# Second attention: a pair's early shares are multiplied ahead of its context maxima

## The reference, cut to what matters

```python
s_ctx = jnp.einsum('bqgrd,bkgd->bgrqk', qb, kc).astype(F32) * scale
s_win = jnp.einsum('bqgrd,bkgd->bgrqk', qb, kb).astype(F32) * scale
s_win = jnp.where(valid, s_win, -jnp.inf)
p = softmax_with_sink(jnp.concatenate([s_ctx, s_win], axis=-1), sink).astype(v.dtype)
return (jnp.einsum('bgrqk,bkgd->bqgrd', p[..., :C], vc)
        + jnp.einsum('bgrqk,bkgd->bqgrd', p[..., C:], vb))
...
sc = jnp.einsum('bqgrd,bkgd->bgrqk', qc, kc).astype(F32) * scale
pc = softmax_with_sink(sc, sink).astype(vc.dtype)
oc = jnp.einsum('bgrqk,bkgd->bqgrd', pc, vc).reshape(b, C, Q_DIM)
```

## Time and profile before

| what | value |
|---|---|
| median of 3 runs | 1539.41 us (1540.07, 1526.01, 1539.41) |
| profiled execution, its own time | 1540.26 us |
| its span | 1538.5 us |
| mean granted TensorE clock | 0.969 |
| PE, PEld, DVE, ACT, POOL busy | 96%, 81%, 50%, 40%, 19% of the span |
| second attention, 439 to 525 us: PE, DVE, ACT busy | 75.8, 76.1, 64.2 of 86.0 us |

### The profile page before, as it was taken

The page is one execution under the profiler, slowest core; times in us unless marked ns, Lnnn a source line. Parts: engine busy times, 40 slices in busy tenths (PEclk is TensorE's granted clock), DMA queues, the critical chain, the costliest instruction groups (busy, mean ns, idle before and its releaser), DMA issues.

```text
span 1538.5 us, 23050 instructions
## 1 busy us (share of the span) xinstructions
PE 1470.8 (96%) x9543; PEld 1245.8 (81%) x9554; DVE 773.6 (50%) x1281; ACT 616.2 (40%) x1131; POOL 290.3 (19%) x217
## 2 busy tenths in 40 slices
PE   7989999889999999999999999999999899999997
PEld 6969899578855677888888887778998678899997
DVE  6665625346369545223222334764453776455453
ACT  4536444345257533222122223442343464353342
POOL 2002375032000021110011111344600021021111
PEclk9989999889999998999999999999999899999999
DMA  7503554875300124223222232132351153645441
GB/s 226 204 29 110 227 219 144 321 282 224 110 1 1 53 89 187 85 76 128 95 98 93 92 110 115 55 110 103 117 192 56 68 183 136 273 176 207 173 166 48
DMA packets 36127, 206.87 MB, mean 134 GB/s; under 512 B 4968, under 2 KB 9496, under 8 KB 14904
## 3 DMA queue, kind: packets, MB, share of 16 engines
q1 hardware_dynamic: 32832, 199.58, 35.4%
q10 hardware_dynamic: 2376, 3.04, 1.0%
q0 software_dynamic: 816, 2.78, 0.6%
HBM read 202.76 MB, written 2.62 MB: 134 GB/s over the span
## 4 chain that ended last, share of the span: by engine, by line
PE 86%; DVE 7%; ACT 2%; DMA 2%; issue 1%; SPq 0%; POOL 0%; ACTq 0%; DVEq 0%
PE lin L1952 19%; PE lin L1953 18%; PE lin L1954 18%; PE lin L2084 5%; PE modp L2011 2%; PE lin L2641 1%; PE lin L1931 1%; DMA ring<-ada_in 1%; PE lin L2590 1%; PE lin L2375 1%; PE lin L1932 1%; PE lin L1937 1%; PE aux L2517 1%; PE lin L1915 1%; PE lin L2360 1%
## 5 line engine op out<-in xcount | busy, mean ns | idle before, releaser
L636 DVE TENSOR_TENSOR w_split<-ring,w_split 128x1024 fp32r<-128x1024 f32 (+1 forms) x140 | 188.0, 1346 | 364.9 <-ACT w_split L631 364.7
L631 ACT ACTIVATE w_split<-ring 128x1024 fp32r<-128x1024 f32 (+1 forms) x140 | 157.6, 1131 | 392.5 <-PE lin L1954 341.4
L1952 PE MATMUL lin<-hn_hi,w_split 128*128 128x512 f32 (+1 forms) x768 | 265.4, 346 | 0.0
L1954 PE MATMUL lin<-hn_hi,w_split 128*128 128x512 f32 (+1 forms) x768 | 264.1, 344 | 0.0
L1953 PE MATMUL lin<-hn_lo,w_split 128*128 128x512 f32 (+1 forms) x728 | 248.5, 341 | 0.0
L1952 PEld LDWEIGHTS lin<-hn_hi,w_split 128*128 128x128 f32 x768 | 145.6, 190 | 17.5 <-issue 0.5
L1954 PEld LDWEIGHTS lin<-hn_hi,w_split 128*128 128x128 f32 x768 | 145.6, 190 | 17.4
L1953 PEld LDWEIGHTS lin<-hn_lo,w_split 128*128 128x128 f32 x728 | 138.1, 190 | 15.8 <-issue 0.5
L1953 PE MATMUL lin<-hid_split,w_split 128*128 128x512 f32 (+1 forms) x348 | 121.4, 349 | 0.0
L583 POOL TENSOR_TENSOR hn<-hn 128x256 f32<-128x256 f32 (+1 forms) x36 | 43.6, 1212 | 334.1 <-ACT hn L727 333.7
L1952 PE MATMUL lin<-hid_split,w_split 128*128 128x512 f32 (+1 forms) x308 | 105.8, 344 | 0.0
(11 more groups left out here) (486 smaller groups left out, 3140.5 us busy)
## 6 DMA issues: line engine op xcount, KB each, us to landing
ring<-ada_in SPq DMA_DIRECT2D x48, 1024.0 KB, 4.9
ring<-ssm_in_in SPq DMA_DIRECT2D x24, 1024.0 KB, 4.9
ring<-od_in_in SPq DMA_DIRECT2D x12, 1024.0 KB, 5.4
ring<-ffn0a_in_in SPq DMA_DIRECT2D x11, 1024.0 KB, 4.7
ring<-ffn0b_in_in SPq DMA_DIRECT2D x11, 1024.0 KB, 4.7
ring<-ffn1a_in_in SPq DMA_DIRECT2D x11, 1024.0 KB, 6.8
ring<-ffn1b_in_in SPq DMA_DIRECT2D x11, 1024.0 KB, 5.0
ring<-ev_in_in SPq DMA_DIRECT2D x9, 1024.0 KB, 13.3
```

Of the source, the lines that this page charges most:

```text
L631: act.activation(parts[:, 0], w, ACT.Copy).then_inc(sig("w_high"), 1)
L636: dve.tensor_tensor(parts[:, 1], w, parts[:, 0].bitcast(F32), ALU.subtract).then_inc(sig("w_low"), 1)
L1952: mm(lin[0:m, tile % RING, 0:width], hi, x_hi, start=kt == 0, stop=False)
L1954: ins = mm(lin[0:m, tile % RING, 0:width], lo, x_hi, start=False, stop=kt == kts - 1)
```

## The change

In the loop of `second_block_vector`, two calls change places. In turns 1 to 7 VectorE waits for the exponentials of part 1 and multiplies the early parts by their shares first, and then waits for the context scores and takes their maxima. Pair 0, ahead of the loop, keeps its order.

```diff
--- before.py
+++ after.py
@@ -1256,8 +1256,8 @@
                 if i > 1:
                     output_parts(i - 2)
                 if i < AT_PAIRS:
+                    shares(i, 0)
                     pair_maxima(i, 2)
-                    shares(i, 0)
                 if 6 <= i < 9:
                     weights_lo(dve, "w_o", i - 6)
             output_parts(AT_PAIRS - 1)
```

## The result

The changed kernel takes 1550.87 us (median of 4 runs, 1544.39 to 1552.61) against 1536.63 us for the kernel before (4 runs, 1526.01 to 1540.07): a ratio of 1.011, 95% interval 1.0071 to 1.015 (the recorded ratio; that of the two medians is 1.009). It is slower by about 1%.

The account below looks back on a forecast made before the run. The prediction took a chain 86% TensorE as the bound, with 5.5 us of waits for VectorE in the second attention. It summed 1540.26 + 9.0 (order) + 0.5 (clock) = 1549.8 us, left at 1549.5, range 1535 to 1562.

Parts of the forecast that it names:

- M2: VectorE's maxima of the context scores, `pair_maxima(i, 2)`, which release ScalarE's context exponentials; the change puts early shares ahead of them.
- S1: TensorE's part 1 scores; the next pair's may not be written before the context exponentials end, sharing their PSUM banks.
- The loop of 11.26 us: Second attention, steady turn: scores, output product, its VectorE parts, shares, maxima and exponentials in series, 11.26 us against 10.18.
- S2: TensorE's context scores, for which VectorE waited 0.67 us a turn ahead of the maxima in the old order.
- The start: First turns of the second attention: part 1 scores of pair 2 late by 1.66 us, of pair 3 by 3.3.
- The sum of the order, +9.0: Second attention: delay the new order adds up to the last pair's exponentials, +8.7 to +9.2 us, taken as +9.0.
- The clock, +0.5: Clock effects at the first turns (-0.4 to +1.65 us) and last output product (0 to +1.0), together taken as +0.5.
- the sum has no clock loss in steady turns: Steady turns: 1.8 us of TensorE idle costs no clock, as after 1.79 us idle in the weight stages; 0 us.
- the clock falls in every turn: Rival: each turn's idle lowers TensorE's clock, 2.4 us a turn, +12 in five turns, 1562 us; chance 0.17.
- an O of over 4 us in the middle turns: Sign of being wrong: TensorE's output product of a pair taking over 4 us in middle turns, pointing to the clock rival.
- Faster: Rival: TensorE's 5.5 us of waits for VectorE go and nothing replaces them, 1534.8 us; chance 0.05.
- washed out: Rival: turns stay near 10.2 to 10.6 us, 9 us of loss becomes 1 to 5, 1541 to 1545 us; chance 0.12.

Follow-up runs that it names:

- e1: Kernel before, with the early shares ahead of the context maxima in turn 4 alone: 1533.97 us in one run, stretch 80.15 us against 77.19.
- e4: Kernel before, with only head 0's part of the early shares put ahead of the context maxima in turns 1 to 7: 1537.29 us, ratio 1.0046.
- e5: Changed kernel, with TensorE's context scores also made one step earlier, as in e3: 1548.54 us, ratio 1.0096 to the kernel before.
- e2: Changed kernel, with TensorE making head 0's eight early transposes twice in six turns: 1541.45 us, ratio 1.0076 to the kernel before.
- e3: Kernel before, VectorE order kept, with TensorE's context scores ahead of the turning of head 1's early parts: 1524.88 us, ratio 0.9962.
- e6: Changed kernel measured and profiled again, no edit: 1546.42 us against 1531.36 us for the kernel before, ratio 1.0082.

## Why the prediction was right, and where it was off

**The side and the place: shown.** M2 is the step that cannot wait. e1 moves it back once and gets S1 late by 1.4 us, never made up; e4 moves it back by 1.2 us of shares instead of 2.0 and gets 10.46 us a turn instead of 11.26.

**The loop of 11.26 us: shown.** The steady turn at full clock is 11.26 us in the changed kernel and in e5, and 11.25 in e2, with 1.90 us of idle time ahead of S1 where 1.8 was forecast. That S2 and the turning are outside it, e5 shows; that they are inside the old one, e3.

**The start: right.** S1 of pair 2 was to be 1.66 us late. It started at 455.54, which is 1.63 us late once the earlier begin of 0.87 us is added. S1 of pair 3 was to be 3.3 us late and was, counted from the start of the stretch, 3.6 late, and 3.3 in e2.

**The sum of the order, +9.0: right**, 8.9 to 9.7 us by e2, where the clock stays up in the loop. e2 also repeats transposes, but in idle time: its turns are as long as the sum without them. S1 of pair 7, forecast at +7.6, came at +7.8 in e2 (and at +12.7 in the changed kernel, with the clock's loss in it).

**The clock, +0.5: mis-sized.** It measured 4.9 us between e2 and the changed kernel, and 4.8 as what is left of 13.8 us when 9.0 are taken off. The bounds for the start were right in kind: the first output product took 3.4 us. So was the lower bound, 0, for the last one: 4.48 us against 4.46, in spite of the longer wait. What failed is the step "the sum has no clock loss in steady turns", drawn from the one idle of 1.79 us ahead of 1009.58. One such row was not enough to carry over to an idle that comes back in each turn; what sets the two apart no run shows. With idles of 1.90 us, three of the five products of pairs 1 to 5 were slow, which is also one of the prediction's own signs of being wrong ("an O of over 4 us in the middle turns"). The rival "the clock falls in every turn" was wrong as well, as the products of pairs 2 and 5 took 2.81 us in both profiles of this kernel. The truth lay between the forecast and that rival: 4.85 us over five turns, about 1.0 a turn and not 2.4. Two turns lost nothing, and in the slow ones S1, which the rival priced at 0.8 us, lost 0 to 0.35. The pattern that the Trainium skill describes in "TensorE: Matmul & The Clock Gate", section "A second HAM failure mode: psum-queue depth-cycling", was there: a clock that swings between its levels behind short idles. The trace agrees with it (0.65 and 1.00 in two turns of the same loop); that the PSUM banks are the reason, no run here shows.

**What lies around the stretch.** The forecast of 1549.5 us stands 1.4 from the measured 1550.87, closer than its terms deserve, by luck. The stretch cost 4.3 us more than the sum of 9.5; the head and the tail were 0.87 and 0.6 us shorter in the profiled execution than in that of before, differences of a size that other executions also show and that I do not explain. The median of the kernel before, too, moved from 1539.41 to 1536.63 with a fourth run: the forecast was +10 us, and the medians differ by 14.2 (15.1 in the measurement of e6). The weight wait that I bounded at -1.45 to 0 hardly moved, from 1.45 to 1.34 us (ahead of 592.65). Of the chances, 0.73 stood on a change within 1% and 0.24 on slower by more; ratios of 1.011 and 1.0082, each with an interval that reaches over 1.01, do not say which it was.

**Faster, and washed out: both fell.** TensorE's old wait did go, in full, and S1's bank dependency took more than it gave back.

**What stays open.** Which idle lowers the clock. Idles of 1.90 us were followed by a fall in some turns and not in others, at places that repeated; 2.21 us was in e1; but in e2 an idle of 2.27 us ahead of S1 of pair 3 was followed by a product of 2.81 us, and in e3 one of 2.38 us by scores at 1.00. Length alone does not decide, and no run separates what else does.

## What to carry to other kernels

Before an instruction is put in front of another, follow the one that is pushed back: here the 0.67 us of idle time ahead of the maxima looked like room for 2 us of shares, but the maxima release the exponentials, and these release a PSUM bank that TensorE was to need 0.2 us later. Add up the loop that the new order closes, link by link, and compare it with the old period; in the changed order and in that of e4 the sum was good to 0.02 us a turn. To remove a short wait in a loop that is nearly balanced, look first for work that can be made ready earlier on the engine that has it (e3), and price any new idle of TensorE of about 2 us with a possible fall of its clock.

## What the runs showed of the hardware

In the changed kernel, idles of only 1.90 us, once in 11 to 13 us, were followed in three of five turns by stretches at a mean granted clock of 0.62 to 0.68, and each slow output product cost 1.2 to 1.7 us. The fall came with some delay: S1 right behind the idle still ran at 1.00 in one of them. With the idle cut to 1.02 us by repeating transposes, the clock stayed at 1.00 in all turns of the loop, and the kernel with more work was the quicker one in the stretch. With idles of 1.10 us and no added work (e4) it stayed at 1.00 as well. The places of the slow products repeated exactly over two executions, 91.00 and 91.03 us in all.
